# A PEER layer's u product: hi and lo parts from the first gate block on

## The chip, the core and the metric

The kernel runs on one core of a Trainium2 chip. The metric is device time in microseconds, the median of several executions. Engines are named as in the profile: PE is TensorE, DVE VectorE, ACT ScalarE, POOL GpSimd, SP the engine that issues most of the DMAs.

## The reference

The program is a small network: two layers (retention and a recurrent mixer, each with a SwiGLU feed-forward), and then a block with a token mixer and a PEER feed-forward. All is f32, for 256 tokens of width 1024. Only PEER's last part matters here. Each token picks 8 x 16 of 16384 experts by product keys; an expert is a row of `u` and a row of `v`:

```python
def chunk(args):
    x_c, i_c, g_c = args
    act = jax.nn.gelu(jnp.einsum('chkd,cd->chk', u_tab[i_c], x_c))
    return jnp.einsum('chk,chkd->cd', g_c * act, v_tab[i_c])
```

where `g_c` is the softmax over the token's 16 picks of each head. `u_tab` and `v_tab` are 16384 x 1024 each, 64 MB.

## The kernel before

The kernel doesn't gather. It multiplies every row of `u` with every token, in 128 blocks of 128 rows ("u stage"), keeps gelu of the products in a table `act_table` of 128 partitions x 128 blocks x 256 tokens (`GT`), multiplies the table by gates that are zero where a token didn't pick the expert, and multiplies the table with `v` in 128 more blocks ("v stage").

Everything in the u stage is written out in Python by `u_steps`, which every engine calls with its own functions, so that the order of each engine's queue is the order of the calls:

```python
def u_steps(first, second, beside=None, last=None):
    first(0)
    for j in range(P):
        if j + 1 < P:
            first(j + 1)
        ...
        second(j)
        if beside:
            beside(j)
```

The parts of a block j, with their lines:

- SP (L901, `load_u`) loads 128 rows of u in four DMAs of 128 KB into one of two buffers `u_rows`. Block j+2 is loaded when block j has been transposed.
- DVE, as `first` (`u_low`): `turn_u(j + 1)` (L2145) transposes block j+1 in 32 x 32 squares, the squares being put in place by the DMA. Since `u_steps` calls `first(j + 1)` in step j, DVE transposes block j+2 in step j.
- PE, as `second` (`activations`, L2725): below block `PARTED` 8 matmuls in full f32, 128 x 128 by 128 x 256, each shown as two records in the trace. They read `u_turned` or `u_turned_more`, four buffers in turn (`plain_buffer`, j modulo 4). From block `PARTED` on 8 x 3 matmuls in the type f32r (L2204 to L2206 in `mm3`): hi x hi, hi x lo, lo x hi, from two buffers each of `u_hi` and `u_lo`.
- ACT, as `first` (`u_high`, L1460), from `PARTED` on: `u_hi`, the f32r part of the transposed block. It waits until PE has finished the block two before (`s_ap`), and never starts before all plain blocks are done, since `u_hi` lies where `input_t`, the plain form's left operand, is.
- DVE, in `u_low` (L2157), from `PARTED` on: `u_lo`, the block less its hi part, once `u_hi` is there. The transposed blocks then have two buffers.
- ACT, as `second` (`gelu`): gelu of the product (L1480). For tokens whose gates are already there the result goes to `gelu_beside` (L1478), and POOL multiplies it into the table (`gate_block`, L1044).

Beside these runs the making of gates. In steps 0 to 45 (`PICKS`, 46 steps) DVE finds the picks of the tokens. From step `GROUP_FIRST` = 49 on, for 64 steps, each step makes the gates of four tokens (`GROUPS` = 64): in step j DVE makes one-hot rows for group j-49 (L2169, after u_steps' `first`), ACT scales four of the eight by the token's gates (`gates_in`, L1468, after gelu and after the copies of an older group), PE multiplies them a step later (L2766, 4 matmuls of 128 x 128), ACT copies the result from PSUM to `gates` and `act_table` (`gates_out`, L1489 and L1490), and POOL multiplies it into the blocks of the table that are there already (`gate_four`, L1051). The one-hots have two buffers.

In step j of a parted block DVE's queue is thus: transpose j+2, u_lo j+1 (waits for u_hi j+1), one-hots j. ACT's is: u_hi j+1, gelu j, gates_out, gates_in j (waits for one-hots j).

```python
GROUPS = S // 4
GROUP_FIRST = len(PICKS) + 3
PARTED = GROUP_FIRST + GROUPS
```

So `PARTED` is 113: blocks 0 to 112 are multiplied plainly, 113 to 127 in parts. The last group's one-hots (step 112) come after `u_lo` of block 113.

Of the kernel before, what the change touches and what calls it, by code (L numbers as in the profile page):

```python
# [352 lines left out]

GROUPS = S // 4
GROUP_FIRST = len(PICKS) + 3
PARTED = GROUP_FIRST + GROUPS


def plain_buffer(j):

    return j % 4


def parted(j):

    return (j - PARTED) // 2 + 1

# [57 lines left out]
def first_and_second_block(nc, A, consts, out, mods, upto=99):  # L425
    cols = lambda name: consts[:, CONST_AT[name][0]:sum(CONST_AT[name])]
    with ExitStack() as ctx:
# [637 lines left out]
        def _(act):  # L1065
# [387 lines left out]
            def u_high(j):  # L1453

                if j < PARTED:
                    return
                b = j % 2
                act.wait_ge(s_ut[b], j // 2 + 1)
                act.wait_ge(s_ap, max(j - 1, PARTED))
                nc.scalar.activation(UTH[:, b, :, :], UT[:, b, :, :], ACT.Copy).then_inc(s_uh[b], 1)  # L1460
# [70 lines left out]
        def _(dve):  # L1531
# [599 lines left out]
            def turn_u(j):  # L2131

                b = j % 2
                dve.wait_ge(s_ur[b], 64 * (j // 2) + 64)
                if j < PARTED:
                    dst = UF[plain_buffer(j)]
                    if j >= 4:
                        dve.wait_ge(s_ap, j - 3)
                else:
                    dst = UT[:, b]  # L2140
                    if j < PARTED + 2:
                        dve.wait_ge(s_ap, max(m for m in range(j) if m < PARTED and plain_buffer(m) == b) + 1)
                    else:
# [666 lines left out]
```

## Time and profile before

| | us |
|---|---|
| median of 3 runs (lowest, highest) | 2286.87 (2285.64, 2291.26) |
| span of the profiled execution | 2288.8 |
| before block 49 is done, from the start of the span | about 1592 |
| blocks 50 to 112, each with a group of gates | 1592 to 1868 |
| parted tail, blocks 113 to 127 | 1868 to 1917 |
| v stage and end | 1917 to 2289 |

The profile is one execution, and its span is 1.9 us above the median of the runs. Times in its rows count from the start of the span. The granted TensorE clock is 0.964 in the mean of the span. "Idle before" is the time that an engine did nothing before the instruction, and behind the arrow stands what released it. Durations of instructions that follow each other overlap a little, so steps are measured from start to start.

### The profile page before, as it was taken

Reading aid. Unit: us, or ns where it says so; the run is one execution under the profiler, and the core shown is the slowest. Engines: PE = TensorE matmul, PEld = TensorE weight load, DVE = VectorE, ACT = ScalarE, POOL = GpSimd, SP = SyncE. Lnnn points to the kernel's source line nnn. Section 1 sums busy time; section 2 is a strip of 40 time slices with the busy share of each in tenths; the row PEclk is TensorE's granted clock in tenths of the full one; section 3 lists DMA queues with packets and bytes.
Section 4 is the critical chain, followed back from the end, with each engine's and each line's share of the span. In section 5 each row is a group of like instructions: output and inputs, shape, how many; then the busy total and the mean of one; then the engine's idle time right before and its main releaser. Section 6 shows DMA issues by size and latency. Waiting matters only on the chain.

```text
span 2288.8 us, 34365 instructions
## 1 busy us (share of the span) xinstructions
PE 2108.4 (92%) x12479; PEld 1839.2 (80%) x12479; DVE 1375.4 (60%) x2074; ACT 959.0 (42%) x1885; POOL 234.4 (10%) x219
## 2 busy tenths in 40 slices
PE   6999899977899999879999879999999999999996
PEld 6876788877798879868888778777999988777775
DVE  5535677677766662154544555998555566666665
ACT  4443433458543443133333332112554454555554
POOL 2101000001000000200000000000345551000000
PEclk9999999998999999969999989999999999999998
DMA  7542566644547853300000453444434345666664
GB/s 251 184 183 91 198 236 222 221 148 148 202 159 259 278 184 106 92 29 1 1 1 8 123 109 98 135 137 148 127 122 120 120 120 185 192 187 190 191 187 135
DMA packets 212839, 333.49 MB, mean 146 GB/s; under 512 B 23654, under 2 KB 141148, under 8 KB 212584
## 3 DMA queue, kind: packets, MB, share of 16 engines
q1 hardware_dynamic: 209320, 321.20, 44.2%
q0 software_dynamic: 3392, 10.52, 1.3%
q8 instruction: 89, 1.46, 0.3%
q14 instruction: 38, 0.31, 0.0%
HBM read 330.58 MB, written 1.08 MB: 145 GB/s over the span
## 4 chain that ended last, share of the span: by engine, by line
PE 68%; DVE 16%; PEld 7%; ACT 3%; issue 3%; DMA 1%; SPq 1%; PEldq 1%; DVEq 0%; ACTq 0%
PE psum L2204 14%; PE psum L2205 14%; PE psum L2206 14%; PE psum L2725 10%; PEld psum L2204 2%; PEld psum L2205 2%; PE psum L2766 2%; PEld psum L2206 2%; DVE weights_lo L1546 2%; PE psum L2616 2%; PE psum L2622 2%; DVE u_turned L2145 1%; DVE u_turned_more L2145 1%; PE psum L2597 1%; DVE top_at L2079 1%
## 5 line engine op out<-in xcount | busy, mean ns | idle before, releaser
L1546 DVE TENSOR_TENSOR weights_lo<-weights,weights_hi 128x1024 fp32r<-128x1024 f32 (+2 forms) x336 | 345.3, 1085 | 261.9 <-ACT weights_hi L1078 257.0
L2204 PE MATMUL psum<-input_hi,weights_hi 128*128 128x256 f32 x1288 | 371.6, 289 | 19.1 <-DVE weights_lo L1546 6.1
L2205 PE MATMUL psum<-input_lo,weights_hi 128*128 128x256 f32 x1288 | 367.8, 286 | 0.0
L2206 PE MATMUL psum<-input_hi,weights_lo 128*128 128x256 f32 x1288 | 367.5, 285 | 0.0
L1078 ACT ACTIVATE weights_hi<-weights 128x1024 fp32r<-128x1024 f32 (+2 forms) x336 | 289.2, 931 | 178.3 <-PEq L2251 117.3
L2204 PEld LDWEIGHTS psum<-input_hi,weights_hi 128*128 128x128 f32 x1288 | 250.7, 195 | 34.6 <-issue 32.8
L2205 PEld LDWEIGHTS psum<-input_lo,weights_hi 128*128 128x128 f32 x1288 | 250.9, 195 | 0.0
L2206 PEld LDWEIGHTS psum<-input_hi,weights_lo 128*128 128x128 f32 x1288 | 250.6, 195 | 0.0
L2725 PE MATMUL psum<-input_t,u_turned 128*128 128x256 f32 x912 | 208.3, 383 | 5.5 <-DVE u_turned L2145 3.3
L2725 PE MATMUL psum<-input_t,u_turned_more 128*128 128x256 f32 x896 | 203.2, 381 | 5.3 <-DVE u_turned_more L2145 3.8
L2204 PE MATMUL psum<-v_hi,act_hi 128*128 128x512 f32 x512 | 203.7, 398 | 0.0
L2205 PE MATMUL psum<-v_lo,act_hi 128*128 128x512 f32 x512 | 199.9, 390 | 0.0
L2206 PE MATMUL psum<-v_hi,act_lo 128*128 128x512 f32 x512 | 199.9, 390 | 0.0
L2725 PEld LDWEIGHTS psum<-input_t,u_turned 128*128 128x128 f32 x912 | 170.6, 191 | 32.7 <-issue 6.3
L2725 PEld LDWEIGHTS psum<-input_t,u_turned_more 128*128 128x128 f32 x896 | 166.4, 190 | 31.8 <-ACT act_table L1480 7.2
L2169 DVE TENSOR_TENSOR one_hots<-param_rows,picks_t 128x1024 f32<-128x1024 f32 x64 | 80.6, 1259 | 115.1 <-PE psum L2766 115.1
L1051 POOL TENSOR_TENSOR act_table<-act_table,gates 128x208 f32<-128x208 f32 (+31 forms) x64 | 111.6, 1743 | 250.1 <-ACT act_table L1490 249.1
L2181 DVE TENSOR_TENSOR act_lo<-act_table,act_hi 128x256 fp32r<-128x256 f32 x128 | 54.9, 429 | 136.0 <-ACT act_hi L1518 136.0
L2204 PEld LDWEIGHTS psum<-v_hi,act_hi 128*128 128x128 f32 x512 | 96.0, 187 | 37.3 <-issue 14.5
L1518 ACT ACTIVATE act_hi<-act_table 128x256 fp32r (+1 forms) x128 | 53.4, 418 | 165.8 <-PE psum L2206 165.8
L2145 DVE STREAM_TRANSPOSE u_turned<-u_rows 128x1024 f32<-128x1024 f32 x72 | 89.2, 1240 | 44.5 <-ACT peer_scores L1319 29.1
L2206 PEld LDWEIGHTS psum<-v_hi,act_lo 128*128 128x128 f32 x512 | 96.1, 188 | 21.2
(381 smaller groups left out, 3921.9 us busy)
## 6 DMA issues: line engine op xcount, KB each, us to landing
u_rows<-in_peer_u_dram SPq DMA_DIRECT2D x512, 128.0 KB, 2.5
weights<-in_ffn_w_in_dram SPq DMA_DIRECT2D x44, 1024.0 KB, 7.7
v_rows_even<-in_peer_v_dram SPq DMA_DIRECT2D x64, 512.0 KB, 3.6
v_rows_odd<-in_peer_v_dram SPq DMA_DIRECT2D x64, 512.0 KB, 3.6
weights<-in_ret_w_in_dram SPq DMA_DIRECT2D x24, 1024.0 KB, 7.4
ada_rows_in<-in_ada_w_dram SPq DMA_DIRECT2D x24, 1024.0 KB, 5.3
weights<-in_ffn_w_out_dram SPq DMA_DIRECT2D x44, 512.0 KB, 6.5
weights<-in_lru_w_in_dram SPq DMA_DIRECT2D x12, 1024.0 KB, 6.4
```

The source lines that it names most:

```text
L1051: nc.gpsimd.tensor_tensor(at_, at_, GE[:, g % 2, :, 0:blocks].rearrange("p t n -> p n t"), ALU.mult)\
L1078: nc.scalar.activation(whi[:, r, at_], wraw[:, r, at_], ACT.Copy).then_inc(s_whi[r], 1)
L1518: nc.scalar.activation(AH[:, j % 2:j % 2 + 1, :], GT[:, bass.ds(4 * i + j, 1), :], ACT.Copy)\
L1546: ins = nc.vector.tensor_tensor(wlo[:, r, at_], wraw[:, r, at_], whi[:, r, at_].bitcast(F32), ALU.subtract)
L2145: nc.vector.transpose(dst.rearrange("p k (c e) -> p c k e", c=4), UR[:, b, :].rearrange("p (c k j) -> p c k j", c=4, k=KT)).then_inc(s_ut[ ...
L2169: nc.vector.tensor_tensor(ONE[:, g % 2], iota, places, ALU.is_equal).then_inc(s_oh, 1)
L2181: nc.vector.tensor_tensor(AL[:, b:b + 1, :], GT[:, bass.ds(4 * i + j, 1), :], AH[:, b:b + 1, :].bitcast(F32), ALU.subtract).then_inc(s_as, 1)
L2204: nc.tensor.matmul(o, ah, bh, start=start, stop=False)
L2205: nc.tensor.matmul(o, ah, bl, start=False, stop=False)
L2206: return nc.tensor.matmul(o, al, bh, start=False, stop=stop)
L2616: ins = nc.tensor.matmul(quarter(j), AM[d][:, j // 2, j % 2, :], XX[d][:, j // 2, j % 2, :], start=True, stop=True)
L2725: ins = nc.tensor.matmul(PS[:, 2 + b, 0:S], UF[plain_buffer(j)][:, k, :], HT[:, k, :], start=k == 0, stop=k == KT - 1)
```

## The change

One constant changes. `PARTED` goes from 113 to 49, so blocks 49 to 127 are multiplied in parts, and the 64 steps in which gates are made all have u_hi, u_lo and the three products. Blocks 0 to 48 stay plain. One-hots and their products stay as they are.

```diff
 GROUPS = S // 4
 GROUP_FIRST = len(PICKS) + 3
-PARTED = GROUP_FIRST + GROUPS
+PARTED = GROUP_FIRST
```

VectorE's queue where the first one-hots stand (steps 48 to 51), before: transposes alternate with one-hots.

```order
L2126 TENSOR_TENSOR picks<-pick_values,gate_sums 128x128
L2145 STREAM_TRANSPOSE u_turned<-u_rows 128x4x8x32 x2
L2145 STREAM_TRANSPOSE u_turned_more<-u_rows 128x4x8x32 x2
L2169 TENSOR_TENSOR one_hots<-param_rows,picks_t 128x1024
L2145 STREAM_TRANSPOSE u_turned<-u_rows 128x4x8x32
L2169 TENSOR_TENSOR one_hots<-param_rows,picks_t 128x1024
```

The same place in the changed kernel:

```order
L2126 TENSOR_TENSOR picks<-pick_values,gate_sums 128x128
L2145 STREAM_TRANSPOSE u_turned<-u_rows 128x4x8x32 x3
L2157 TENSOR_TENSOR u_lo<-u_turned,u_hi 128x1024
L2145 STREAM_TRANSPOSE u_turned<-u_rows 128x4x8x32
L2157 TENSOR_TENSOR u_lo<-u_turned,u_hi 128x1024
L2169 TENSOR_TENSOR one_hots<-param_rows,picks_t 128x1024
```

From here on to step 112 the three stand in the order transpose, u_lo, one-hots in every step; u_lo is new, in front of the one-hots.

ScalarE's queue in steps 51 and 52, before (the first row ends a step):

```order
L1468 ACTIVATE one_hots<-one_hots,picks_t 128x128 x4
L1480 ACTIVATE act_table<-psum 128x256
L1489 ACTIVATE gates<-psum 128x4x52
L1490 ACTIVATE act_table<-psum 128x4x76
L1468 ACTIVATE one_hots<-one_hots,picks_t 128x128 x4
L1478 ACTIVATE gelu_beside<-psum 128x4
```

and in the changed kernel:

```order
L1468 ACTIVATE one_hots<-one_hots,picks_t 128x128 x4
L1460 ACTIVATE u_hi<-u_turned 128x1024
L1480 ACTIVATE act_table<-psum 128x256
L1489 ACTIVATE gates<-psum 128x4x52
L1490 ACTIVATE act_table<-psum 128x4x76
L1468 ACTIVATE one_hots<-one_hots,picks_t 128x128 x4
L1460 ACTIVATE u_hi<-u_turned 128x1024
```

The u_hi is new, behind the four scalings of the step before and in front of the gelu.

## Rows read from the trace of the kernel before

**Rows 1.** The page's engine line: busy us, share of the span, instructions

```profile
PE 2108.4 (92%) x12479; PEld 1839.2 (80%) x12479; DVE 1375.4 (60%) x2074; ACT 959.0 (42%) x1885; POOL 234.4 (10%) x219
```

**Rows 2.** Windows: stretch, length, PE, PEld, DVE, ACT, POOL busy, PEclk, DMA share, GB/s

```profile
1592.00:1868.00 276.00, 274.51 (x1516) 248.22 (x1514) 153.19 (x129) 139.21 (x502) 133.84 (x122) 1.00 0.40 121
...
1868.20:1916.90 48.70, 45.84 (x368) 44.63 (x369) 38.63 (x34) 23.72 (x44) 16.93 (x18) 1.00 0.57 176
```

**Rows 3.** Timeline, one middle step: start, length, engine, instruction, idle before and releaser

```profile
1700.28 1.05 PE L2766 MATMUL psum<-one_hots 128*128 128x128 f32 x8
1700.48 0.25 ACT L1478 ACTIVATE gelu_beside<-psum 128x92 f32<-128x92 f32 x1 [2.13 <-PE psum L2725]
...
1701.17 3.62 PE L2725 MATMUL psum<-input_t,u_turned_more 128*128 128x256 f32 x16
1701.37 1.23 DVE L2169 TENSOR_TENSOR one_hots<-param_rows,picks_t 128x1024 f32<-128x1024 f32 x1 [1.97 <-PE psum L2766]
1701.43 1.26 ACT L1468 ACTIVATE one_hots<-one_hots,picks_t 128x128 f32<-128x128 f32 x4
...
1702.52 1.24 DVE L2145 STREAM_TRANSPOSE u_turned_more<-u_rows 128x1024 f32<-128x1024 f32 x1
...
1704.63 1.05 PE L2766 MATMUL psum<-one_hots 128*128 128x128 f32 x8
```

**Rows 4.** Timeline, where the hi and lo form begins (block 113)

```profile
1865.71 1.06 ACT L1460 ACTIVATE u_hi<-u_turned 128x1024 fp32r<-128x1024 f32 x1 [2.26 <-PE psum L2725]
1865.73 1.25 DVE L2145 STREAM_TRANSPOSE u_turned<-u_rows 128x1024 f32<-128x1024 f32 x1 [6.48 <-PE psum L2725]
...
1866.89 1.18 DVE L2157 TENSOR_TENSOR u_lo<-u_turned,u_hi 128x1024 fp32r<-128x1024 f32 x1
...
1867.18 1.47 POOL L1044 TENSOR_TENSOR act_table<-act_table,gelu_beside 128x244 f32<-128x244 f32 x1 [3.31 <-ACT act_table L1480]
1867.42 0.28 ACT L1490 ACTIVATE act_table<-psum 128x60 f32<-128x60 f32 x1
1868.00 1.73 DVE L2169 TENSOR_TENSOR one_hots<-param_rows,picks_t 128x1024 f32<-128x1024 f32 x1
...
1868.22 0.36 PE L2204 MATMUL psum<-input_hi,u_hi 128*128 128x256 f32 x1 [1.72 <-DVE u_lo L2157]
...
1868.61 2.42 POOL L1051 TENSOR_TENSOR act_table<-act_table,gates 128x452 f32<-128x452 f32 x1
...
1869.76 1.28 ACT L1468 ACTIVATE one_hots<-one_hots,picks_t 128x128 f32<-128x128 f32 x4 [2.05 <-DVE one_hots L2169]
...
1870.95 1.04 ACT L1460 ACTIVATE u_hi<-u_turned 128x1024 fp32r<-128x1024 f32 x1
...
1872.02 1.23 DVE L2157 TENSOR_TENSOR u_lo<-u_turned,u_hi 128x1024 fp32r<-128x1024 f32 x1 [1.14 <-ACT u_hi L1460]
```

**Rows 5.** Timeline, the first one-hots, before GpSimd has begun

```profile
1592.35 1.18 DVE L2169 TENSOR_TENSOR one_hots<-param_rows,picks_t 128x1024 f32<-128x1024 f32 x1
...
1593.57 1.28 ACT L1468 ACTIVATE one_hots<-one_hots,picks_t 128x128 f32<-128x128 f32 x4 [0.47 <-DVE one_hots L2169]
```

**Rows 6.** Timeline of POOL, its product with the gelu, narrow and wide

```profile
1605.38 0.20 POOL L1044 TENSOR_TENSOR act_table<-act_table,gelu_beside 128x4 f32<-128x4 f32 x1 [2.14 <-ACT act_table L1480]
...
1861.83 0.70 POOL L1044 TENSOR_TENSOR act_table<-act_table,gelu_beside 128x240 f32<-128x240 f32 x1 [1.39 <-ACT act_table L1480]
```

**Rows 7.** Timeline of ACT, two gelus in the hi and lo tail

```profile
1898.94 0.38 ACT L1478 ACTIVATE gelu_beside<-psum 128x256 f32<-128x256 f32 x1 [1.68 <-PE psum L2206]
...
1901.81 0.39 ACT L1478 ACTIVATE gelu_beside<-psum 128x256 f32<-128x256 f32 x1 [1.54 <-PE psum L2206]
```

**Rows 8.** Timeline around blocks 48 to 51

```profile
1589.26 0.39 ACT L1480 ACTIVATE act_table<-psum 128x256 f32<-128x256 f32 x1 [2.69 <-PE psum L2725]
1591.18 1.25 DVE L2145 STREAM_TRANSPOSE u_turned_more<-u_rows 128x1024 f32<-128x1024 f32 x1 [2.42 <-DMA u_rows<-in_peer_u_dram]
...
1596.85 3.62 PE L2725 MATMUL psum<-input_t,u_turned_more 128*128 128x256 f32 x16
```

## The prediction

> **What bounds the kernel now.** I read the busy shares of the whole page first. TensorE is busy for 92% of the span, VectorE for 60% and ScalarE for 42% [rows 1]. That suggests that work moved from TensorE to the other two is a gain. It is an average, so I next cut out the stage that the change touches, by stretches of time: from 1592 to 1868 us TensorE is busy 274.51 of 276.00 us, VectorE 153.19 and ScalarE 139.21 [rows 2]. Here TensorE sets the pace, and nothing else is near it.
>
> Then the instructions of one step in order of time [rows 3]. I call a step j what the engines do for block j of 128 rows of u. The gate product of one step starts at 1700.28 us, the u product after it at 1701.17 and the next gate product at 1704.63: 4.35 us a step, 0.89 for the gates and 3.46 for u. VectorE idles 1.97 us before the one-hots, ScalarE 2.13 us before the gelu. By sums there is room: u_lo would need about 1.2 us of VectorE a step, u_hi 1.05 of ScalarE.
>
> Last, the place where the kernel already does what the change spreads out: at 1865.7 us, block 113, the parted form begins while one group of one-hots is still to be made [rows 4]. It is the only full step in which both happen, and it is the row that the forecast rests on: from the u_hi at 1865.71 to the next u_hi at 1870.95 are 5.24 us, more than the 4.35 of a plain step.
>
> **The change part by part.** Blocks 49 to 112, 64 of them, go from 16 recorded f32 passes to 24 hi and lo products. The parted tail gives TensorE's time for such a block: the gelus at 1898.94 and 1901.81 us are 2.87 apart [rows 7]. With the gate product's 0.89 TensorE needs 3.76 us a step, 0.59 less than now. Added are one u_hi on ScalarE (1.05) and one u_lo on VectorE (1.2) a step. The transpose stays, and so do the loads of u, with two landing buffers as before.
>
> What decides is the order. In front of each one-hots instruction VectorE now has u_lo of the block after it, and in front of each u_hi ScalarE has the four scalings of the one-hots. So u_hi(j+1) releases u_lo(j+1); behind that in VectorE's queue stands one-hots(j); this releases the scalings (j); and behind these in ScalarE's queue stands u_hi(j+2). That is a closed ring over one step, with no product of TensorE in it. Four pieces of it are in the rows:
> u_hi to u_lo: 1870.95 to 1872.02, 1.07 us (the 1.18 after 1865.71 had a transpose before it).
> u_lo to one-hots: 1866.89 to 1868.00, 1.11 us; there the u_lo took 1.18, while one that was waited for takes 1.23, so I use 1.16.
> One-hots to scalings: 1592.35 to 1593.57, 1.22 us, with GpSimd quiet [rows 5].
> Scalings to the next u_hi: 1869.76 to 1870.95, 1.19 us.
> The ring takes 4.64 us a step, before GpSimd. It is longer than TensorE's 3.76 and than the 4.35 of now.
>
> Gelu and the two copies of gates out of PSUM stand between u_hi and the scalings on ScalarE. The last of them ends at 1867.70 in rows 4 (1867.42 and 0.28), and the scalings wait until 1869.76, so they cost nothing. The transpose (1.23) runs under the scalings and u_hi (2.26), with 1.0 us left. The u product starts 1.33 us after u_lo starts (1866.89 to 1868.22), is over 3 us later, and is wanted only by the u_hi of two blocks on: hidden. TensorE will wait some 0.9 to 1.5 us a step for u_lo.
>
> GpSimd adds to the ring. At 1867.18 us its product with the gelu was issued while u_lo ran, took 1.47 us instead of the 0.70 of its neighbour [rows 6], and the one-hots that followed took 1.73 us instead of 1.18: 0.55 lost in the ring, 0.15 less than GpSimd's own 0.70. The second product of GpSimd then waited for the one-hots, 2.42 us in all, and ran beside the transpose, which was not lengthened. The first product grows from 0.20 us at width 4 (block 52) to 0.70 at 240 (block 111) [rows 6]. Taking the same 0.15 off, the delay grows from 0.05 to 0.55, 0.30 in the mean, over 60 steps: 18.0 us. The bounds of this term are nothing and 0.55 in each step, 0 to 33 us (not below nothing, since the 4.64 has no GpSimd in it); I take the line between, since both ends of the width are in rows.
> The Trainium skill, SBUF — State Buffer, section Who interferes with whom, says that a VectorE instruction with two SBUF inputs and a GpSimd instruction that reads SBUF exclude each other for the whole instruction, whichever issued first. The rows agree in kind. By that rule the whole 0.20 to 0.70 would count, 27 us in place of 18, and the time would be 9 us longer; the one-hots' 1.73 us is the measured case and decides.
>
> The sum over steps. Block 51's product starts at 1596.85 [rows 8], block 113's at 1868.22 [rows 4]: 271.4 us for 62 steps now, with the 1.9 us halt at the switch at its end. In the changed kernel these are 62 x 4.64 = 287.7, and 18.0, so 305.7: 34.3 more.
>
> The switch moves to block 49 and costs there. The first u_hi must wait until block 48 has been multiplied, which is at the gelu of 1589.26 [rows 8]. From there, by the same pieces: u_lo(49) at 1590.4, the transpose of 51 at 1591.7, u_lo(50) at 1592.9, one-hots at 1594.0, scalings at 1595.2, u_hi(51) at 1596.4, u_lo(51) at 1597.4, product of 51 at 1598.8. That is 1.9 us later than now. Rows of u aren't late: the rows of 51 were there at 1591.18.
> After block 113 both kernels run the same: one last one-hots beside block 114, then the parted tail, then the v stage.
>
> The sum: 34.3 + 1.9 = 36.2 us more. The profiled execution has a span of 2288.8 us, so its like would have 2325; it is 1.9 above the median of the runs, 2286.87, and against that I forecast 2323.
>
> **The rivals.** A: TensorE keeps the pace. If the one-hots aren't held up behind u_lo, a step takes TensorE's 3.76: 62 x 3.76 = 233.1, which is 38.3 less than 271.4; with the 1.9 of the switch 2250. For it speak the idle times of rows 3; it decides from the point where the ring is under 3.76 us, and the ring's four measured pieces are 4.64 without GpSimd. The Trainium skill, FP8 and Floating Point Precision, section TensorE Precision Notes, gives true FP32 four passes, so three products would take three quarters, 2.60 in place of 2.87; by that this rival would stand 17 us lower still, but the trace's 2.87 is used.
> B, faster as well: the ring goes through TensorE over two blocks and not through the one-hots: u product 3.46 and 0.20 to its gelu (1700.28 to 1700.48) less the 0.59 saved, 3.1; gelu to the end of the scalings 2.2 (1700.48 to 1702.69) [rows 3]; u_hi 1.07; u_lo to product 1.33: 7.7 for two blocks, 3.85 a step. 62 x 3.85 = 238.7, so 2256. It would hold if VectorE had the one-hots ahead of u_lo. The order says otherwise.
> C: the ring holds, but GpSimd yields each time, and its first product waits out both VectorE instructions. Then the 18 us go: 2305. Against it is the 1.73 us in rows 4, one observation late in the stage.
> D: GpSimd's second product gets in front of the one-hots too. Free of waiting it took about 1.3 us at 1869.73 (2.42 less the wait), and about 0.6 in proportion to its width early: 60 steps at 1.0, so 2383. It is issued after the first product ends, when the one-hots already wait; in rows 4 the one-hots won.
> E: the change is carried out but makes no difference, the ring being equal to 4.35 by chance: 2287 to 2290.
>
> **How the numbers follow.** Forecast 0.77, A 0.03, B 0.03, C 0.10, D 0.05, E 0.02. The forecast's pieces are read to 0.05 us, four of them over 62 steps: plus or minus 8 us; the GpSimd term can be off by as much as a third, 6. I say 2309 to 2335, which takes in the page's rule (2332) and stops short of C. Faster by over 0.3% (about 7 us, what a measurement of this kernel can tell from no change) 0.06, within it 0.02, slower 0.92.
>
> **What the new profile would show.** Right: steps of 4.7 us after 1600 us growing to 5.2 near the end of the stage; TensorE idle about 1 us a step, released by u_lo; ScalarE's scalings released by the one-hots, and u_lo released by u_hi; the one-hots' mean at 1.5 us and not 1.26. TensorE's total busy time lower by some 38 us. Wrong: steps of 3.8 with TensorE full (A, B); one-hots at 1.2 us throughout with steps of 4.65 (C); one-hots over 2 us (D). A lower granted clock in TensorE's gaps would make it wrong in another way; now it is 1.00, the upper level of 2.4 GHz, in both stretches of rows 2, the second with gaps in it.

## The result and the profile after

| | us |
|---|---|
| before, median of 4 | 2287.01 (2285.64 to 2291.26) |
| changed, median of 4 | 2324.16 (2319.48 to 2327.10) |
| ratio | 1.0154, 95% interval 1.0138 to 1.0170 |
| span of the profiled execution, before and changed | 2288.8 and 2321.0 |

Forecast were 2323 us and 36 more than before; measured are 2324.16 and 37 more. In spans the difference is 32.2 us, since the profiled execution of the changed kernel reached block 48 three microseconds earlier (1586.3 us, [rows 8] has 1589.3), in a stretch that the change doesn't touch.

The page of the changed kernel, its engine line and four groups (columns as in the page: busy us, mean ns of one, then idle before and its releaser):

```profile
PE 2080.7 (90%) x12991; PEld 1828.3 (79%) x12991; DVE 1461.1 (63%) x2138; ACT 1026.2 (44%) x1949; POOL 295.5 (13%) x219
...
L2204 PE MATMUL psum<-input_hi,u_hi 128*128 128x256 f32 x632 | 184.7, 292 | 60.6 <-DVE u_lo L2157 60.1
...
L1051 POOL TENSOR_TENSOR act_table<-act_table,gates 128x208 f32<-128x208 f32 (+31 forms) x64 | 131.5, 2055 | 232.9 <-ACT act_table L1490 232.9
...
L2157 DVE TENSOR_TENSOR u_lo<-u_turned,u_hi 128x1024 fp32r<-128x1024 f32 x79 | 97.6, 1236 | 79.0 <-ACT u_hi L1460 78.8
...
L1468 ACT ACTIVATE one_hots<-one_hots,picks_t 128x128 f32<-128x128 f32 x256 | 82.1, 392 | 103.7 <-DVE one_hots L2169 103.7
```

TensorE has 28 us less to do than in [rows 1], VectorE 86 and ScalarE 67 more. The idle times carry the result: TensorE stood 60.1 us before the first of the u products, released by u_lo, and ScalarE stood 103.7 us before the scalings, released by the one-hots.

The same stretch as [rows 2] and parts of it (columns as there):

```profile
1592.00:1870.00 278.00, 229.24 (x1833) 220.01 (x1831) 211.46 (x172) 185.96 (x510) 172.38 (x110) 1.00 0.36 109
...
1600.00:1700.00 100.00, 84.79 (x681) 81.41 (x680) 75.39 (x64) 70.64 (x191) 57.89 (x41) 1.00 0.37 111
...
1800.00:1900.00 100.00, 79.82 (x638) 76.53 (x636) 77.17 (x60) 63.27 (x179) 70.42 (x40) 1.00 0.33 102
```

In [rows 2] TensorE was busy 274.51 of 276.00 us; now 229.24 of 278. No engine is full: VectorE, the next, has 77% at most. The busy shares would not tell what the bound is. The waits of 1600 to 1900 us do (who waited for whom, total us, times, longest), and then the chain of what ended last, from 1700 to 1712 us:

```profile
ACT one_hots L1468 <- DVE one_hots L2169: 100.0, 61, 2.0
DVE u_lo L2157 <- ACT u_hi L1460: 70.8, 62, 1.1
...
PE psum L2204 <- DVE u_lo L2157: 54.1, 61, 1.1
```

```profile
by line: DVE one_hots L2169 33.0%; DVE u_lo L2157 30.6%; ACT one_hots L1468 16.7%; ACT u_hi L1460 16.0%; issue 5.2%; ACTq L1477 0.3%
...
1704.79 1.22 DVE u_lo L2157
1706.01 1.32 DVE one_hots L2169
1707.33 0.02 issue
1707.35 0.03 ACT one_hots L1468
...
1707.66 0.98 ACT one_hots L1468 x3
1708.64 0.96 ACT u_hi L1460
1709.60 0.02 issue
1709.62 1.22 DVE u_lo L2157
```

The chain (start, us, what) is the ring of the prediction, one turn in 4.83 us: u_lo, one-hots, scalings, u_hi, u_lo. TensorE, which had 3.46 of 4.35 us of each step in [rows 3] for u alone, is not in it at all.

Two turns in order of time, an early and a late one (the changed kernel's timeline, columns as in [rows 3]):

```profile
1609.94 1.22 DVE L2157 TENSOR_TENSOR u_lo<-u_turned,u_hi 128x1024 fp32r<-128x1024 f32 x1 [1.14 <-ACT u_hi L1460]
...
1610.33 0.90 POOL L1044 TENSOR_TENSOR act_table<-act_table,gelu_beside 128x8 f32<-128x8 f32 x1 [2.05 <-ACT act_table L1480]
...
1611.08 1.22 DVE L2169 TENSOR_TENSOR one_hots<-param_rows,picks_t 128x1024 f32<-128x1024 f32 x1
...
1612.34 1.28 ACT L1468 ACTIVATE one_hots<-one_hots,picks_t 128x128 f32<-128x128 f32 x4 [1.28 <-DVE one_hots L2169]
...
1613.53 1.04 ACT L1460 ACTIVATE u_hi<-u_turned 128x1024 fp32r<-128x1024 f32 x1
...
1614.60 1.23 DVE L2157 TENSOR_TENSOR u_lo<-u_turned,u_hi 128x1024 fp32r<-128x1024 f32 x1 [1.15 <-ACT u_hi L1460]
```

```profile
1889.22 1.22 DVE L2157 TENSOR_TENSOR u_lo<-u_turned,u_hi 128x1024 fp32r<-128x1024 f32 x1 [1.15 <-ACT u_hi L1460]
...
1889.59 1.41 POOL L1044 TENSOR_TENSOR act_table<-act_table,gelu_beside 128x236 f32<-128x236 f32 x1 [1.41 <-ACT act_table L1480]
...
1890.36 1.71 DVE L2169 TENSOR_TENSOR one_hots<-param_rows,picks_t 128x1024 f32<-128x1024 f32 x1
...
1890.96 2.39 POOL L1051 TENSOR_TENSOR act_table<-act_table,gates 128x444 f32<-128x444 f32 x1
...
1892.11 1.28 ACT L1468 ACTIVATE one_hots<-one_hots,picks_t 128x128 f32<-128x128 f32 x4 [2.00 <-DVE one_hots L2169]
...
1893.29 1.04 ACT L1460 ACTIVATE u_hi<-u_turned 128x1024 fp32r<-128x1024 f32 x1
...
1894.37 1.22 DVE L2157 TENSOR_TENSOR u_lo<-u_turned,u_hi 128x1024 fp32r<-128x1024 f32 x1 [1.14 <-ACT u_hi L1460]
```

Early the ring takes 4.66 us (1609.94 to 1614.60), late 5.15 (1889.22 to 1894.37). All of the difference lies between u_lo's start and the scalings' start, 2.40 us early and 2.89 late, and there in the one-hots, 1.22 and 1.71 us. GpSimd's first product was issued beside u_lo in both. Late it is still at work for some 0.5 us when u_lo has ended, and the one-hots wait; its second product then waits for them.

### The profile page after: what moved, and what is told of

It reads as the page before. It is cut to its first block, busy times and chain, and to the rows that moved or that the text cites. A ratio compares the mean times of both kernels' runs of the same rounds, so it can differ in the third digit from the quotient of the medians.

```text
span 2321.0 us, 35581 instructions
## 1 busy us (share of the span) xinstructions
PE 2080.7 (90%) x12991; PEld 1828.3 (79%) x12991; DVE 1461.1 (63%) x2138; ACT 1026.2 (44%) x1949; POOL 295.5 (13%) x219
## 4 chain that ended last, share of the span: by engine, by line
PE 55%; DVE 22%; ACT 8%; PEld 7%; issue 4%; DMA 2%; SPq 1%; PEldq 1%; ACTq 0%; DVEq 0%; POOL 0%
PE psum L2204 14%; PE psum L2206 14%; PE psum L2205 14%; DVE one_hots L2169 4%; DVE u_lo L2157 4%; ACT one_hots L1468 3%; ACT u_hi L1460 3%; PEld psum L2204 2%; PEld psum L2205 2%; PEld psum L2206 2%; PE psum L2616 2%; PE psum L2622 2%; DVE weights_lo L1546 1%; DVE u_turned L2145 1%; DVE u_turned_more L2145 1%
## 5 line engine op out<-in xcount | busy, mean ns | idle before, releaser
L2204 PE MATMUL psum<-input_hi,u_hi 128*128 128x256 f32 x632 | 184.7, 292 | 60.6 <-DVE u_lo L2157 60.1
L2205 PE MATMUL psum<-input_lo,u_hi 128*128 128x256 f32 x632 | 179.3, 284 | 0.0
L2206 PE MATMUL psum<-input_hi,u_lo 128*128 128x256 f32 x632 | 179.2, 284 | 0.0
L2204 PEld LDWEIGHTS psum<-input_hi,u_hi 128*128 128x128 f32 x632 | 121.1, 192 | 72.2 <-issue 70.1
L1051 POOL TENSOR_TENSOR act_table<-act_table,gates 128x208 f32<-128x208 f32 (+31 forms) x64 | 131.5, 2055 | 232.9 <-ACT act_table L1490 232.9
L2145 DVE STREAM_TRANSPOSE u_turned<-u_rows 128x1024 f32<-128x1024 f32 x104 | 128.5, 1237 | 39.6 <-ACT peer_scores L1319 29.1
L2157 DVE TENSOR_TENSOR u_lo<-u_turned,u_hi 128x1024 fp32r<-128x1024 f32 x79 | 97.6, 1236 | 79.0 <-ACT u_hi L1460 78.8
L1468 ACT ACTIVATE one_hots<-one_hots,picks_t 128x128 f32<-128x128 f32 x256 | 82.1, 392 | 103.7 <-DVE one_hots L2169 103.7
```

The lines of the kernel that those rows point to most:

```text
L1051: nc.gpsimd.tensor_tensor(at_, at_, GE[:, g % 2, :, 0:blocks].rearrange("p t n -> p n t"), ALU.mult)\
L1468: ins = nc.scalar.activation(one, one, ACT.Copy, scale=HKT[:, 2, t:t + 1])
L2145: nc.vector.transpose(dst.rearrange("p k (c e) -> p c k e", c=4), UR[:, b, :].rearrange("p (c k j) -> p c k j", c=4, k=KT)).then_inc(s_ut[ ...
L2157: nc.vector.tensor_tensor(UTL[:, b, :, :], UT[:, b, :, :], UTH[:, b, :, :].bitcast(F32), ALU.subtract)\
L2204: nc.tensor.matmul(o, ah, bh, start=start, stop=False)
L2205: nc.tensor.matmul(o, ah, bl, start=False, stop=False)
```

## The experiments

Each kernel of the table ran four or five times, beside runs of the kernel before on the same chip (medians 2290.07, 2289.32 and 2288.52 us in the three sittings).

| kernel | us | ratio to before (95%) | a step, from u_hi to u_hi |
|---|---|---|---|
| changed, again | 2325.90 | 1.0155 (1.0138 to 1.0172) | 4.66 to 5.16 |
| two products in place of three | 2325.61 | 1.0164 (1.0129 to 1.0200) | 4.65 to 5.16 |
| parted from block 81 on | 2308.97 | 1.0090 (1.0073 to 1.0107) | 4.89 to 5.16, from there |
| first GpSimd product on one column | 2308.18 | 1.0082 (1.0062 to 1.0101) | 4.66 flat |
| one-hots before u_lo | 2265.76 | 0.9896 (0.9857 to 0.9934) | 3.74 and 4.02 in turn, later 4.1 |
| both orders turned | 2263.31 | 0.9893 (0.9859 to 0.9928) | 3.8 at first, then 4.2 to 4.5, in the one profiled |
| u_hi ahead | 2259.36 | 0.9877 (0.9843 to 0.9911) | 3.77 to 4.03 |
| u_hi ahead, first product narrow | 2255.58 | 0.9846 (0.9830 to 0.9862) | 3.77 to 4.0 |
| u_hi ahead, both products narrow | 2251.37 | 0.9847 (0.9815 to 0.9879) | 3.77 flat |

**The one-hots first.** The ring has four links, and two of them are only the order of a queue. This takes VectorE's:

```diff
             def u_low(j):
...
                     turn_u(j + 1)
+                if group_made(j - 1) is not None:
+                    one_hot_rows(group_made(j - 1))
                 if j >= PARTED:
...
                 picks_step(j)
-                if group_made(j) is not None:
-                    one_hot_rows(group_made(j))
```

> The changed kernel with VectorE's order turned in the gate steps: transpose of j+2, one-hots j, then u_lo j+1, so that the one-hots no longer stand behind u_lo. ScalarE's order stays. Ring theory (u_hi, u_lo, one-hots, scalings, u_hi): it is cut, and what is left is the loop over two blocks of rival B, product to gelu 3.1, gelu to the end of the scalings 2.2, u_hi 1.07, u_lo to product 1.33: 3.85 us a step, so about 2256 to 2264 us. Rival, VectorE and GpSimd are simply too full (the same instructions are left): steps stay at 4.7 to 5.2 and the time at 2324. TensorE theory: no change.

Measured 2265.76 us, 2 over the range. The same instructions, in another order, are some 58 us faster than the changed kernel: they weren't too many. Steps alternate between 3.74 and 4.02 us early on, 3.88 in the mean. That is close to the 3.85 of the loop over two blocks, but it is not that loop. Its first window and its chain from 1620 to 1650 us:

```profile
1600.00:1700.00 100.00, 99.48 (x821) 97.40 (x821) 97.24 (x78) 81.59 (x230) 30.32 (x49) 1.00 0.45 135
```

```profile
by line: DVE one_hots L2171 36.9%; DVE u_turned L2145 33.2%; DVE u_lo L2159 31.1%; issue 1.7%; DVEq L2144 0.5%
```

The chain has VectorE alone in it, busy for 97%, and from 1600 to 1840 us u_lo waits for u_hi once, 1.2 us. The three instructions of a step, with one-hots of 1.3 and 1.6 us in turn, make up the 3.74 and 4.02; alone these take 1.22, and the rest fits GpSimd holding them up.

**u_hi ahead.** This takes ScalarE's link instead: u_hi of block j+2 is issued right after the gelu of block j, in front of the gates' copies and the scalings.

```diff
-            def u_high(j):
+            def u_high(j, ahead=False):

-                if j < PARTED:
+                if j < PARTED or (j >= PARTED + 2) != ahead:
                     return
...
             def gelu(j):
...
                 ins.then_inc(s_ag, 1)
+                if PARTED <= j < P - 2:
+                    u_high(j + 2, True)
```

> Only ScalarE's order is turned (u_hi of j+2 directly behind the gelu of j); VectorE keeps u_lo before the one-hots. Ring theory: one cut in the ring is enough, so it falls too: steps of 3.8 to 4.1, 2252 to 2270 us. If the wait of the one-hots behind u_lo were the cost by itself, and not the ring, it would stay near 2324.

Measured 2259.36 us, the fastest version that computes everything, and faster than both kernels. VectorE's order is that of the changed kernel, with the one-hots behind u_lo; so that wait costs nothing by itself, and only the closed ring did. Its windows and its chain:

```profile
1600.00:1700.00 100.00, 100.00 (x844) 99.88 (x843) 100.00 (x79) 84.01 (x236) 55.35 (x51) 1.00 0.46 138
1700.00:1800.00 100.00, 100.00 (x825) 98.55 (x824) 100.00 (x78) 81.88 (x231) 61.75 (x52) 1.00 0.45 134
```

```profile
by line: DVE u_lo L2159 41.1%; DVE u_turned L2147 34.5%; issue 26.0%; DVE one_hots L2171 1.6%
...
1702.84 1.23 DVE u_turned L2147
1704.07 1.60 DVE u_lo L2159
1705.67 0.06 DVE one_hots L2171
1705.73 1.00 issue
```

In these windows TensorE and VectorE are both busy all the time, and steps start at TensorE's 3.77 us. The chain runs in VectorE's u_lo and transposes. u_lo takes 1.54 and 1.60 us there: it is held up too, by GpSimd.

**Both orders.** The two edits together.

> As the run with the one-hots before u_lo, and ScalarE's u_hi of block j+2 put directly behind the gelu of block j, ahead of the copies of gates and the scalings. Ring theory: neither loop is left, the next bounds are TensorE's 3.76 us and, late in the stage, the instructions of VectorE and GpSimd that exclude each other: u_lo 1.15, one-hots 1.15, GpSimd 0.9 at first and 2.1 at the end, 3.2 to 4.4. Mean step 3.8 to 3.95: 2252 to 2262 us. Rival (load, not order): 2324 as before.

Measured 2263.31 us, 1 above its range and no better than one cut alone. In the one profiled execution (2283.26 us, the others 2260.71 to 2264.08) steps were 4.2 to 4.5 us. Its rows (GpSimd's second product, one-hots, u_lo):

```profile
1805.17 1.27 POOL L1051 TENSOR_TENSOR act_table<-act_table,gates 128x400 f32<-128x400 f32 x1 [0.57 <-ACT act_table L1492]
...
1805.42 2.11 DVE L2173 TENSOR_TENSOR one_hots<-param_rows,picks_t 128x1024 f32<-128x1024 f32 x1
...
1807.45 1.21 DVE L2161 TENSOR_TENSOR u_lo<-u_turned,u_hi 128x1024 fp32r<-128x1024 f32 x1
```

GpSimd's second product is issued just before the one-hots, and these take 2.11 us: with this order the exclusion falls in the other way round, and VectorE waits for the longer product. Early in the stage it was u_lo that was held up, with 1.8 to 2.0 us. Why this execution was 20 us over the others isn't shown; the others have no profile.

**Less work on TensorE.** In the changed kernel u_hi x input_lo is left out in blocks 49 to 112.

```diff
+                        if j < GROUP_FIRST + GROUPS:
+                            nc.tensor.matmul(PS[:, 2 + b, 0:S], UTH[:, b, k, :], HH[:, k, :], ...)
+                            ins = nc.tensor.matmul(PS[:, 2 + b, 0:S], UTL[:, b, k, :], HH[:, k, :], ...)
+                            continue
                         ins = mm3(...)
```

> The changed kernel with the product u_hi x input_lo left out in blocks 49 to 112, so that TensorE has 16 passes in place of 24 there (the output is less exact). Ring theory: TensorE isn't in the ring, steps stay at 4.66 to 5.16, TensorE only waits longer, 2324 us within 2. If TensorE's product or its f32r form set the pace, 64 x 8 x 0.12 = 61 us less, 2263.

Measured 2325.61 us, the changed kernel's time. Its windows show TensorE with some 15 us less to do in each 100 than the changed kernel and nothing gained:

```profile
1600.00:1700.00 100.00, 69.43 (x509) 62.41 (x510) 76.07 (x65) 69.86 (x188) 56.63 (x41) 1.00 0.37 113
1700.00:1800.00 100.00, 68.33 (x494) 61.61 (x492) 76.88 (x62) 66.70 (x185) 65.12 (x41) 0.98 0.36 107
```

(The 0.98 is TensorE's clock, at half for 3.4 us from 1758 on.) Steps are those of the changed kernel. So no price of the f32r products is in the 37 us, and rival A, TensorE keeping the pace, had no ground in this order.

**Parted from the middle on.** `PARTED = GROUP_FIRST + GROUPS // 2`.

> The parted form from block 81 on, in the middle of the gate stage (before: 113, changed: 49). Ring theory: 31 steps at 4.35 as before, then 31 steps of the ring at 4.91 to 5.16 as the changed kernel's trace has them (156.1 us, where the plain form has 134.7): 21 us over before, 2308. If the loss were one of the switch at block 49, or of TensorE's products evenly, it would be at 2324 or at half of it, 2306; the steps tell: flat 4.35 up to 1735 us, then at once 4.9.

Measured 2308.97 us, 2308 forecast. The first window is the plain form, the second, from some 1718 us on, the parted one, in one execution:

```profile
1600.00:1700.00 100.00, 100.00 (x554) 90.50 (x553) 54.78 (x48) 51.71 (x185) 41.32 (x47) 1.00 0.39 121
1700.00:1800.00 100.00, 83.03 (x626) 78.80 (x625) 70.86 (x57) 62.02 (x179) 63.26 (x41) 1.00 0.34 102
```

Steps go from 4.35 to 4.89 us where the form changes (1715 to 1720 us), and follow the changed kernel's to 5.16. The profiled execution was the fastest of its four, 2301.39 us, and the others took 2308.36 to 2312.18. Its steps are no shorter for that: it reached the first one-hots at 1581.1 us, where the kernel before has 1592.4 [rows 5], so the difference lies ahead of the gate stage. By the total alone the two theories named, 2308 and 2306, could not have been told apart.

**GpSimd's first product.**

```diff
-                at_ = GT[:, j, 0:n]
-                nc.gpsimd.tensor_tensor(at_, at_, GB[:, c % 2, 0:n], ALU.mult).then_inc(s_gb, 1)
+                at_ = GT[:, j, 0:1]
+                nc.gpsimd.tensor_tensor(at_, at_, GB[:, c % 2, 0:1], ALU.mult).then_inc(s_gb, 1)
```

> The changed kernel with GpSimd's first product (table block by gelu_beside) cut to one column, so that the table isn't multiplied in the rest of them; everything else is left. If this product's wait sits in the ring, the one-hots stay at about 1.2 us and steps at 4.66 throughout, and the 15.1 us by which the 63 steps of the changed kernel exceed 4.66 go: 2309. If the growth had another cause (the wider second product, ScalarE's wider copies), steps would still grow to 5.16: 2324.

Measured 2308.18 us and 4.66 us in every step to the end, the one-hots at 1.22 throughout. From the first one-hots to the last it took 294.97 us, the changed kernel 309.64: 14.7 less. Late in the stage:

```profile
1885.01 0.89 POOL L1044 TENSOR_TENSOR act_table<-act_table,gelu_beside 128x1 f32<-128x1 f32 x1 [1.39 <-ACT act_table L1480]
...
1885.76 1.22 DVE L2169 TENSOR_TENSOR one_hots<-param_rows,picks_t 128x1024 f32<-128x1024 f32 x1
```

The product has one column and still shows 0.89 us, nearly all of it waiting for u_lo. That wait is free. What the ring pays is what is left of the product's own work after u_lo has ended.

**What is left with u_hi ahead.** The same edit on top of u_hi ahead, and then GpSimd's second product on one block too (`GT[:, 0:1, ...]`).

> u_hi of j+2 directly behind the gelu of j, and GpSimd's first product cut to one column as well. With the ring cut, TensorE's 3.77 us and the VectorE-GpSimd exclusion are left; with the first product gone the exclusion is 0.6 to 1.4 us of GpSimd against 2.3 of VectorE, under 3.77 in sum, so steps stay at 3.77 to the end where they grew to 4.03: some 6 us less than with u_hi ahead alone, 2253. If the growth there was the second product's, no change, 2259.

> As the run with u_hi ahead and the first GpSimd product on one column, and the second product (gates into the finished blocks) cut to one block as well, so most of the table isn't multiplied by gates. If the growth of the steps to 4.0 us that stayed is the second product shutting VectorE out, steps are flat at 3.77 to 3.8, TensorE's own, and the time is some 5 us less, 2250. If something else grows (ScalarE's copies, loads), steps still reach 4.0, 2256.

The first gave 2255.58 us, 3.8 less and not 6, and steps still grew to 4.0 us. Even the 3.8 are not clear: the two kernels ran in different sittings, and the intervals of their ratios overlap. From the first one-hots to the last the profiled executions took 245.48 us with u_hi ahead and 245.30 with the first product narrow as well, which is no gain: so the trace gives the time of the rival in the expectation, where the growth is the second product's. Whether narrowing the second product alone would be enough wasn't tried. The hold-up only moved: late in the stage the one-hots fell from 1.7 to 1.21 us, and u_lo rose from 1.3 to between 1.65 and 1.8. My sum of both engines' work had left out the transpose. VectorE's three instructions take 3.5 of the 3.77 us (93.21 of 100 below), so each hold-up of over some 0.3 us lengthens the step.

With both products narrow steps are 3.77 us from the first to the last, and TensorE has no gap:

```profile
1700.00:1800.00 100.00, 100.00 (x852) 100.00 (x851) 93.21 (x81) 83.02 (x241) 17.77 (x53) 1.00 0.47 139
```

That is TensorE's own pace, and 2251.37 us is what rival A had said (2250) for a kernel without ring. From the first one-hots to the last it took 237.62 us, 7.9 less than with u_hi ahead alone: so much VectorE and GpSimd cost by shutting each other out, and it went only with both products narrow.

**The halt at the switch.** 20 matmuls into the bank of the coming product, before the wait for block 49's u_lo:

```diff
+                    for n in range(20 if j == PARTED else 0):
+                        nc.tensor.matmul(PS[:, 2 + b, 0:S], HH[:, n % KT, 0:P], HH[:, n % KT, :], start=True, stop=True)
                     pe.wait_ge(s_ul[b], parted(j))
```

> The changed kernel with 20 matmuls put before block 49's product, where TensorE stands still for 2.6 us waiting for u_lo; their result is overwritten. If the stop is what lets the granted clock fall to 0.50 (from 1589.3 to 1592.7 us), it stays at 1.00 and the block's product takes 2.9 us in place of 4.4, and the switch costs 1.5 us less, too little for the total to show. If the clock falls for another reason, it falls all the same.

In the changed kernel TensorE stands 2.61 us before block 49's product, and its granted clock is at half, 1.2 GHz, for most of that product (timeline row, then windows; the number behind POOL's is PEclk):

```profile
1588.79 0.36 PE L2204 MATMUL psum<-input_hi,u_hi 128*128 128x256 f32 x1 [2.61 <-DVE u_lo L2157]
```

```profile
1590.00:1591.00 1.00, 1.00 (x6) 1.00 (x6) 1.00 (x1) 0.00 (x0) 0.00 (x0) 0.50 0.74 239
...
1593.00:1594.00 1.00, 1.00 (x11) 1.00 (x10) 0.39 (x1) 0.56 (x2) 0.00 (x0) 1.00 0.39 125
```

With the 20 matmuls (first row) the clock stays at 1.00 through block 49's product, which starts at 1591.20 us in this execution:

```profile
1588.34 2.74 PE L2729 MATMUL psum<-input_hi 128*128 128x256 f32 x20
```

```profile
1591.00:1592.00 1.00, 0.87 (x7) 0.80 (x7) 0.89 (x2) 0.13 (x1) 0.00 (x0) 1.00 0.52 137
1592.00:1593.00 1.00, 1.00 (x11) 1.00 (x10) 1.00 (x2) 0.00 (x0) 0.00 (x0) 1.00 0.80 259
1593.00:1594.00 1.00, 1.00 (x11) 1.00 (x10) 1.00 (x2) 0.00 (x0) 0.00 (x0) 1.00 0.57 170
```

From the u_hi of block 49 to that of block 51 are 7.18 us (1.29 and 5.89) instead of 8.61 (1.29 and 7.32). Its one execution took 2324.21 us, which as foreseen can't show it.

That the stop brought the fall fits the other traces, but not each of them. Nine profiled executions have this stop of 2.61 us, and in eight the clock fell behind it. In the ninth, with both orders turned, it stayed at 1.00 from the stop's end on:

```profile
1584.09 0.36 PE L2206 MATMUL psum<-input_hi,u_hi 128*128 128x256 f32 x1 [2.61 <-DVE u_lo L2161]
```

So the stop alone does not decide it, and one execution with matmuls in the stop makes its part likely, not certain.

## Why the prediction was right

**The ring** was forecast from one place of the trace before, four links, 4.64 us a step without GpSimd. The first steps and those of the kernel with a narrow first product took 4.66. What it took to see it was the order of the two queues, [rows 4] and the pieces' start to start times; the busy shares of [rows 1, 2] pointed the other way. Both ways of cutting the ring brought the time from 2324 to 2259 and 2266, so the ring is shown and not argued. The one-hots' mean was put at 1.5 us and is 1.46.

**GpSimd's share** was 18.0 us by a line from 0.05 to 0.55. It was 14.6: 303.6 us for the 62 steps, less 62 x 4.66; the kernel with a narrow first product saved the same, 14.7. The late end was well read (5.16 for 5.19), the early end a little high: the one-hots stay at 1.22 us up to a width of some 12. At width 8 the product's row ends at 1611.23 us and u_lo's at 1611.16, so next to nothing of it is left. The Trainium skill's rule (SBUF — State Buffer, Who interferes with whom), the whole 0.20 to 0.70 of the product, gave 27 and would have missed by 12. The two do exclude each other as it says, but the part of GpSimd's instruction that counts is only what outlasts u_lo; the trace puts that 0.2 us under the instruction's own length.

**The switch** was put at 1.9 us over before and cost 3.5 (from the end of block 48 to the start of block 51's product 11.05 us, before 7.59). The step that failed is that I gave block 49's product its 2.87 us: after a stop of 2.6 us it ran at half the clock and took about 4.4. In the kernel before the halt of 1.7 us at the switch hadn't done this, and the row that I leaned on came from there. One execution of nine had the same stop and kept the full clock, so this term can come out 1.4 us smaller.

**The sum** of 34.3 and 1.9 was 32.2 and 3.5: 35.7 for 36.2. Two terms were off by 2 us each, in opposite directions, so that 2323 lies so near 2324.16 is in part luck.

**What was hidden** was rightly put at nothing: transposes, gelu, gates' copies and loads of u show no wait in the ring. TensorE's busy time fell by 28 us and not by 38. The half clock added some 1.5 us to it; where the rest comes from isn't shown, and nothing in the sum hung on it.

**The rivals.** A (2250) needed the ring gone, and with the ring and GpSimd gone it is 2251.37. B (2256) is near what cutting one link left, 2259 and 2266, but by luck: its loop through TensorE over two blocks shows in neither trace. In both, u_lo hardly waits for u_hi, and the chain runs on VectorE. C and D, GpSimd always or never giving way, are excluded for this order of instructions by the one-hots' slow growth from 1.22 to 1.73 us. Of D's kind, though, is the kernel with both orders turned, where the longer product came first.

## What to carry to other kernels

Before work is moved from a full engine to idle ones, write down the queues of these engines with their waits and look for a closed loop over one step: its length is the sum of its links, and no engine in it needs to be full. Such a loop is often half dependence and half mere order of issue, and one link of order turned (here u_hi before the scalings instead of behind them) turned 37 us lost into 28 gained (the ratio 0.9877). Where a trace holds a single step of the new kind, at a switch or an edge, its start to start times can be the better forecast; here they gave 4.64 us for 4.66, and the busy times 3.76. And when a link is cut, read the chain anew: here VectorE's own instructions came next, and not the loop that was expected.

## What the runs showed of the hardware

- Behind a stop of 2.61 us TensorE's granted clock fell to half (1.2 GHz), 0.6 to 1.2 us after work had begun again, for 3.4 us, and came back while the engine worked. This is so in eight of the nine profiled executions with that stop; in the ninth, and in the one with matmuls in the stop, it stayed at full. Single stops of 1.72 us (before, and parted from block 81 on) and one of 0.7 to 1.1 us in every step of the changed kernel left it at 1.00. With two products in place of three each step had two stops, 1.1 and 0.3 to 0.75 us, and there it fell three times, for 3.4 us each.
- A GpSimd product of one column took 0.89 us behind a VectorE u_lo of 1.23 us, and a VectorE one-hots of 1.22 us took 2.11 us behind a GpSimd product of 1.27. Whichever is under way finishes, so the same pair costs either engine, by order of issue alone.
- With VectorE at 100% busy its steps grew with GpSimd's width although GpSimd was 55 to 62% busy; without the exclusion VectorE needed 93% for a step of 3.77 us.
